# Output projection of a hybrid layer: where its sixteen-plus-sixteen units of work are issued among attention's rounds

## The reference, cut to what matters

```python
proj = h @ w_in[l]                                   # aq, ak, av, bu, bg, cq, ck, cv
out_a = _dilated_mixture(aq, ak, av)                 # 8 heads of 64
out_b = _conformer_conv(bu, bg, conv_w, ...)         # 31 taps over time, 512 channels, layer norm, silu
out_c, _ = _band_attention(cq, ck, cv, 127, sinks)   # 16 heads of 64
mix = concat([out_a, out_b, out_c])                  # 512 + 512 + 1024 = 2048 channels
x = x + mix @ w_out[l]                               # 2048 x 2048
h2 = _rms_norm(x, norm2_g[l])
x = x + (silu(h2 @ w_gate[l]) * (h2 @ w_up[l])) @ w_down[l]
```

## Time and profile before

| | |
|---|---|
| median of 3 runs | 2099.89 us (2097.58 to 2101.59) |
| the profiled execution's own time | 2101.12 us |
| its span, first to last instruction | 2099.4 us |
| mean granted TensorE clock | 0.987 |
| PE busy | 2032.4 us (97% of the span) |
| DVE busy | 1123.7 us (54%) |
| ACT busy | 932.1 us (44%) |
| DMA | 360.79 MB, mean 172 GB/s |

### The profile page before, as it was taken

One profiled execution on the slowest core, in us unless ns is written; L12 is line 12 of the kernel. 1 busy time (PEld: TensorE's weight loads), 2 busy tenths in 40 slices (PEclk: granted clock), 3 DMA queues, 4 the chain that ended last, 5 costly groups with the idle time before them and its releaser, 6 DMA issues.

```text
span 2099.4 us, 28004 instructions
## 1 busy us (share of the span) xinstructions
PE 2032.4 (97%) x10386; PEld 1721.1 (82%) x10386; DVE 1123.7 (54%) x1309; ACT 932.1 (44%) x1215; POOL 77.0 (4%) x126
## 2 busy tenths in 40 slices
PE   8999999998999999999999888999999999999998
PEld 6888988887879998887788766888888888888886
DVE  5474544655555453654656874555444544444443
ACT  5355434444454443444554424454444444433342
POOL 3000000001100000000200100000000000000000
PEclk9999999999999999999999998999999999999999
DMA  8574455565665444565554422566666666656653
GB/s 259 166 241 121 131 159 167 172 199 147 209 196 174 136 141 146 175 200 162 158 170 134 128 90 101 167 205 187 190 188 189 191 188 187 189 191 203 205 202 111
DMA packets 209513, 360.79 MB, mean 172 GB/s; under 512 B 22641, under 2 KB 45728, under 8 KB 209152
## 3 DMA queue, kind: packets, MB, share of 16 engines
q1 hardware_dynamic: 203728, 345.36, 53.7%
q0 software_dynamic: 4816, 13.76, 2.2%
q10 hardware_dynamic: 864, 0.26, 0.1%
HBM read 357.22 MB, written 2.10 MB: 171 GB/s over the span
## 4 chain that ended last, share of the span: by engine, by line
PE 92%; DVE 2%; ACT 2%; DMA 2%; issue 1%; SPq 1%; DVEq 0%; ACTq 0%; POOL 0%; POOLq 0%
PE psum L550 24%; PE psum L552 24%; PE psum L551 24%; PE psum L558 3%; PE psum L560 3%; PE psum L561 3%; PE psum L607 1%; PE psum L1181 1%; SPq L505 1%; PE psum L616 1%; DVE wl L521 1%; PE psum L779 1%; PE psum L856 1%; PE psum L630 1%; ACT wh L514 1%
## 5 line engine op out<-in xcount | busy, mean ns | idle before, releaser
L521 DVE TENSOR_TENSOR wl<-raw,wh 128x1024 fp32r<-128x1024 f32 (+2 forms) x672 | 797.9, 1197 | 734.3 <-ACT wh L514 727.2
L514 ACT ACTIVATE wh<-raw 128x1024 fp32r<-128x1024 f32 (+2 forms) x672 | 690.7, 1037 | 885.5 <-PE psum L552 716.1
L550 PE MATMUL psum<-wh,xh 128*128 128x512 f32 (+2 forms) x1600 | 623.7, 390 | 0.8 <-DVE xl L798 0.6
L552 PE MATMUL psum<-wh,xl 128*128 128x512 f32 (+2 forms) x1600 | 616.8, 385 | 0.0
L551 PE MATMUL psum<-wl,xh 128*128 128x512 f32 (+2 forms) x1600 | 616.4, 385 | 0.0
L550 PEld LDWEIGHTS psum<-wh,xh 128*128 128x128 f32 x1600 | 302.5, 189 | 62.1 <-DVE wl L521 1.9
L552 PEld LDWEIGHTS psum<-wh,xl 128*128 128x128 f32 x1600 | 301.6, 188 | 59.6
L551 PEld LDWEIGHTS psum<-wl,xh 128*128 128x128 f32 x1600 | 302.4, 189 | 57.6
L550 PE MATMUL psum<-wh,mh 128*128 128x512 f32 x384 | 154.0, 401 | 16.7 <-issue 8.5
L552 PE MATMUL psum<-wh,ml 128*128 128x512 f32 x384 | 152.6, 397 | 0.0
L551 PE MATMUL psum<-wl,mh 128*128 128x512 f32 x384 | 152.5, 397 | 0.0
(11 more groups left out here) (340 smaller groups left out, 1550.0 us busy)
## 6 DMA issues: line engine op xcount, KB each, us to landing
raw<-in_w_in_dram SPq DMA_DIRECT2D x264, 512.0 KB, 4.4
raw<-in_w_out_dram SPq DMA_DIRECT2D x96, 512.0 KB, 3.7
raw<-in_w_gate_dram SPq DMA_DIRECT2D x88, 512.0 KB, 3.6
raw<-in_w_up_dram SPq DMA_DIRECT2D x88, 512.0 KB, 3.6
raw<-in_w_down_dram SPq DMA_DIRECT2D x80, 512.0 KB, 3.7
bias<-in_b_in_dram POOLq DMA_DIRECT2D x18, 256.0 KB, 4.0
raw<-in_w_in_dram SPq DMA_DIRECT2D x16, 268.0 KB, 2.8
raw<-in_nsa_cmp_w_k_dram SPq DMA_DIRECT2D x32, 128.0 KB, 2.5
```

Source lines behind the costliest of these rows:

```text
L514: act.activation(wh[:, n % SPLIT_SLOTS, 0:k, 0:unit.n], raw[:, n % RAW_SLOTS, 0:k, 0:unit.n], ACT.Copy).then_inc(hi_done, 1)
L521: dve.tensor_tensor(out=wl[:, n % SPLIT_SLOTS, 0:k, 0:unit.n], in0=raw[:, n % RAW_SLOTS, 0:k, 0:unit.n], in1=wh[:, n % SPLIT_SLOTS, 0:k, 0 ...
L550: pe.matmul(o, ah_[:, kt, tok], hi_w, start=first, stop=False)
L552: ins = pe.matmul(o, al_[:, kt, tok], hi_w, start=False, stop=last)
```

## The change

The order in which the 32 units of `w_out` are issued is new. All four column groups take their pairs 4 to 7 first ("early"), are added to `x`, and take pairs 0 to 3 in a second pass ("late"), which is added to `x` again. Slots 16 to 28 then hold 2, 2, 3, 1, 3, 2, 2, 3, 4, 2, 4, 2 and 2 units, one slot fewer than before; slots 16 to 22 hold 15 and the first of slot 23 is the sixteenth early one. There are eight `add_output` instead of four. In slot 23 the wait for mid 22 is on the second unit, in slot 24 the wait for mid 23 on the first. `turn_final_x` for the last columns moves from stage 28 to 27. The taps of the convolution are spread otherwise (31 before and after), and `head_scale` of the `aq` and `ak` groups moves from mid 11 and 13 to mid 12 and 14, with `sinks_max` put first in mids 11 and 13.

```diff
 def output_slots_2():
-    def unit(g, pair):
-        return output_unit("w_out_2", g, pair, 3, 4)
-    rest = [output_unit("w_out_2", g, pair, 7) for g in (2, 3) for pair in range(8)]
-    slots = [[unit(0, 4)], [unit(0, 5)], [unit(1, 4), unit(1, 5)], [unit(0, 6)], [unit(0, 7), unit(1, 6)], [unit(1, 7)],
-             [], [unit(0, 0), unit(0, 1), unit(1, 0), unit(1, 1)], [unit(0, 2), unit(0, 3)],
-             [unit(1, 2), unit(1, 3), rest[0], rest[1]]]
-    slots[7][0].after_mid = 22
+    def early(g, *pairs):
+        return [output_unit("w_out_2", g, pair, 7, 4) for pair in pairs]
+
+    def late(g, *pairs):
+        return [output_unit("w_out_2", g, pair, 3, 0) for pair in pairs]
+    slots = [early(0, 4, 5), early(1, 4, 5), early(0, 6, 7) + early(1, 6), early(1, 7), early(2, 4, 5, 6),
+             early(2, 7) + early(3, 4), early(3, 5, 6), early(3, 7) + late(0, 0, 1), late(0, 2, 3) + late(1, 0, 1),
+             late(1, 2, 3), late(2, 0, 1, 2, 3), late(3, 0, 1), late(3, 2, 3)]
+    slots[7][1].after_mid = 22
     slots[8][0].after_mid = 23
-    slots[9][2].after_mid = 24
-    return slots + slots_of(rest[2:])
+    return slots
...
-                26: lambda: turn_final_x(range(0, 8)), 28: lambda: turn_final_x(range(8, EARLY_KT)),
+                26: lambda: turn_final_x(range(0, 8)), 27: lambda: turn_final_x(range(8, EARLY_KT)),
...
-                26: lambda: final_x_high(range(0, 8)), 28: lambda: final_x_high(range(8, EARLY_KT)),
+                26: lambda: final_x_high(range(0, 8)), 27: lambda: final_x_high(range(8, EARLY_KT)),
...
-            taps_at_unit = {first_tap_unit + SLOT_UNITS * i + n: 1 for i, m in enumerate((4, 4, 3, 3, 3)) for n in range(m)}
-            taps_at_mid = {9: 2, 15: 3, 16: 4, 17: 2, 18: 3}
+            taps_at_unit = {first_tap_unit + SLOT_UNITS * i + n: 1 for i, m in enumerate((4, 2, 3, 2, 3, 2, 2)) for n in range(m)}
+            taps_at_unit[first_tap_unit + sum(len(slot) for slot in SLOTS_2[11:19])] = 1
+            taps_at_mid = {9: 3, 15: 1, 16: 3, 17: 2, 18: 3}
...
-                11: lambda: (head_sums("aq2", 512), sinks_max("c10", 8), head_scale("aq2", 1, 512, split_heads(aqn)), sinks_sum("c10")),
-                12: lambda: (dve_copy_half(probT2)),
-                13: lambda: (head_sums("ak2", 512), sinks_max("c14", 12), small_out(o_c[1], 0), head_scale("ak2", 0, 512, split_heads(akn)), sinks_sum("c14")),
-                14: lambda: (dve_copy_half(probT2)),
+                11: lambda: (sinks_max("c10", 8), head_sums("aq2", 512), sinks_sum("c10")),
+                12: lambda: (dve_copy_half(probT2), head_scale("aq2", 1, 512, split_heads(aqn))),
+                13: lambda: (sinks_max("c14", 12), small_out(o_c[1], 0), head_sums("ak2", 512), sinks_sum("c14")),
+                14: lambda: (dve_copy_half(probT2), head_scale("ak2", 0, 512, split_heads(akn))),
...
-                17: lambda: (softmax_max("a0"), softmax_sum("a0")), 18: lambda: dve_copy_half(probT2),
-                19: lambda: (softmax_max("a4"), small_out(o_a, 0), softmax_sum("a4")),
-                20: lambda: (dve_copy_half(probT2), conv_mean()), 21: lambda: small_out(o_a, 4),
-                22: lambda: (conv_sumsq(), dve_mix_low(place, "a", mh2, ml2, 0, 0)), 23: conv_low,
-                24: lambda: add_output(0), 25: lambda: add_output(1), 26: lambda: final_x_low(range(0, 8), 1),
-                27: lambda: add_output(2), 28: lambda: final_x_low(range(8, EARLY_KT), 2), 29: last_output,
+                17: lambda: (softmax_max("a0"), softmax_sum("a0")),
+                18: lambda: (dve_copy_half(probT2), add_output(0)),
+                19: lambda: (softmax_max("a4"), small_out(o_a, 0), softmax_sum("a4"), add_output(1)),
+                20: lambda: (dve_copy_half(probT2), conv_mean()), 21: lambda: (small_out(o_a, 4), add_output(2)),
+                22: lambda: (conv_sumsq(), dve_mix_low(place, "a", mh2, ml2, 0, 0)),
+                23: lambda: (conv_low(), add_output(3)),
+                24: lambda: add_output(0), 25: lambda: add_output(1),
+                26: lambda: (add_output(2), final_x_low(range(0, 8), 1)),
+                27: lambda: final_x_low(range(8, EARLY_KT), 2), 28: last_output,
```

## The result

The changed kernel took 2085.54 us, the median of four runs (2084.14 to 2087.65), against 2100.74 for the kernel before: a ratio of 0.9931, 95% interval 0.9918 to 0.9944, or 12 to 17 us less. Measured again on another occasion, with five more runs of it, the ratio was 0.9917 (0.9904 to 0.9931). The forecast was 2085.5.

A forecast was written before the change was run, and what follows sets the result against it. PE, busy 97% of the span, was taken as the bound. Gains and losses at ten places summed to -14.4 us, taking the profiled 2101.12 to 2086.7, or 2085.5 against the median 2099.89; range 2080 to 2093.

The forecast's parts named there:

- (a): Slot 11: a third tap after mid 9 stands ahead of DVE's first split, so PE starts later; 1.7 us lost.
- (b): Stage 12 and slot 13: gap 0.9 us instead of 5.6, clock stays up; loss 8.5 before, 1.5 after.
- (c): Slot 17: its unit's wait and slow work go; 6.4 us lost before, 0 after.
- (d): Stage 18: DVE's work ahead of it outlasts PE's; gap 1.5 us instead of 0.9.
- (e): Slot 19: gap of 3.3 us and slow unit of 2.7 unchanged; mid 18's new addition fits under the slow unit.
- (g): Stage 22: two units now cover mid 21; gap of 1.2 us and about 1.4 of low clock go, gain 2.6.
- (h): Slot 23: its first unit covers mid 22; gap of 2.5 us and 1.9 of slow work go, gain 4.4.
- (i): Slot 24: uncovered mid 23 grows by a fourth split and an addition; gap 8.4 us for 6.0, 2.4 lost.
- (j): Stage 27: slot 27's two units do not cover mid 26, where four did before; 1.3 us lost.
- rival 2: More is won: slot 19's slow unit (2.7 us) may go and slot 11's tap (1.7) cost nothing; 2081, chance 0.09.
- rival 1: DVE, busier by four additions and the moved scaling, is late at more places, giving back 6.2 us; 2092, chance 0.11.
- rival 4: Slower: after the longer gap before slot 24 the clock stays low through slots 24 to 28; 2119 us, chance 0.04.

The follow-up runs named there:

- e6: The changed kernel with the third tap after mid 9 moved into slot 12: 2085.35 us, ratio 0.9925.
- e3: The changed kernel with mids 11 to 14 as before (head_sums ahead of sinks_max, head_scale in mids 11 and 13): 2087.45 us, ratio 0.9942.
- e2: The changed kernel with mids 9 and 11 to 14 and the taps of slots 11 to 15 as before, keeping the new unit order and additions: 2091.18 us.
- e11: The changed kernel without the four early add_output, so the early halves of the output projection are missing: 2082.3 us, ratio 0.9918.
- r1: The changed kernel, unedited, measured again: 2083.14 us, ratio 0.9917.
- e10: The changed kernel with the wait for mid 22 on slot 23's first unit instead of its second: 2088.98 us, ratio 0.9949.
- e4: The changed kernel with slot 24's fourth unit moved to slot 25 and add_output(3) ahead of conv_low: 2083.29 us, ratio 0.9922.
- e7: The changed kernel with the two taps after mid 17 moved to slots 14 and 15: 2084.46 us, ratio 0.9927.
- e5: The changed kernel with early units dealt one each to slots 21 to 23, two to slot 24 before mid 23's wait, add_output(3) in mid 24: 2077.72 us.
- e1: The kernel before with only the change's early part (mids 9 and 11 to 14, taps of slots 11 to 15): 2098.7 us, ratio 0.9984.
- e9: The kernel of e5 with one of slot 24's two early units moved to the end of slot 23: 2080.46 us, ratio 0.9909.

## Why the prediction was right, step by step

The table sets the steps against the two profiles. "Measured" is how much later or earlier PE reached the next mark after the end of stage 10, with 2.72 a unit for units that now lie elsewhere, and then the differences. For example, slot 24 began at 1301.22 - 1136.90 = 164.3 with 12 of the 32 units done, and after at 1299.25 - 1136.65 = 162.6 with 18: -1.7 - 6 x 2.72 = -18.0, where the mark before it (stage 22) stood at -14.2.

| step, up to the mark | predicted | measured |
|---|---|---|
| (a), (b): to stage 13 | -5.3 | -4.3 |
| (c): to stage 17 | -6.4 | -6.6 |
| (d): to stage 18 | +0.6 | +0.4 |
| (e): to stage 19 | 0 | -1.7 |
| (f), (g): to stage 22 | -2.6 | -2.0 |
| (h), (i) and the clock from stage 22 on: to slot 24 | -2.0 | -3.9 |
| (j) and slots 24 to 28: to the last turn of x | +1.3 | +1.3 |
| sum | -14.4 | -16.7 |

Sorted by kind, the sum forecast 7.3 us less of standing still and 7.1 us less of slow or DVE-paced work. The two windows of the stretch show 7.1 and 9.7. So the gaps, which are what the edit sets, came out as forecast, and what was mis-sized is nearly all clock.

**(a)** held in size (a gap of 1.57 for 1.7). It stands in the sum as a cost beside (b), whose gap it shortens by as much, so the total is right; but there is nothing to win by undoing it. e6 shows this: DVE sets stage 12, and a tap ahead of it costs the same wherever it stands. So the second gain of rival 2, 1.7 us from this tap, was not there.

**(b)** held in its gap, 0.95 for 0.9, and the clock stayed up. Its pace in slot 13 was mis-sized: from stage 12 to stage 13 PE took 14.89 us before and 13.50 after, 1.4 gained for 2.3 in the sum. DVE's pace, put at 0.6, cost about 1.1. Part of this is a new wait on `wl` before the first unit of slot 13, small, but one of the signs that the prediction named for being wrong:

```profile
1166.99 0.50 PE L552 MATMUL psum<-wh,xh 128*128 128x512 f32 x1 [0.35 <-DVE wl L523]
```

The cover claimed for `head_scale` held too, since e3 undoes the move and no gap of slots 14 to 18 shrinks.

**(c)** held in result, and its working was a little too dark. DVE was expected 1.5 late at mid 15; it waited 0.22 for stage 15:

```profile
1211.54 0.88 DVE L1665 TENSOR_TENSOR o_c<-psum,small 128x128 f32<-128x128 f32 x4 [0.22 <-PE psum L1297]
...
1214.03 1.68 DVE L757 SCALAR_TENSOR_TENSOR conv_y<-conv_h,conv_wT,conv_y 128x256 f32<-128x256 f32 x4
1215.78 1.23 DVE L523 TENSOR_TENSOR wl<-raw,wh 128x1024 fp32r<-128x1024 f32 x1
```

Most of that came from mid 13, which the sum had not used: it ended at 1192.7 for 1198.6 before, 5.9 earlier, where PE's stage 13 came only 4.6 earlier. e2 shows that (c) and what follows stand without the early part.

**(d)** came out at 1.41 for 1.5. **(e)** was mis-sized: the gap is 3.26 as forecast, but the slow unit was charged as certain, and in the profile of after it did not come (granted clock 1.00). With the unit at full clock PE was at stage 19 before mid 18 was done, the 0.66; the addition that was to hide under the slow unit showed, and e11 without it has no such gap. In r1 the unit was slow and the gap gone. This is rival 2's first half, by luck of the execution and not by the schedule.

**(g), (h)** held in their gaps, which are gone. e10 brings (h) back: a gap of 2.53 and a clock of 0.68 over 5.21 us of matmuls, 1.7 lost, together 4.2 for the 4.4 forecast (its stretch is 3.8 longer, as the clock behind slot 24's gap came back sooner in that execution). **(i)** held: 8.20 for 8.4, and e4 and e11 take its two halves out again, 2.07 together and 1.14 the addition. ACT and then DVE in the profile after show the chain as forecast, the fourth split ahead of the table load and the addition behind `conv_low`:

```profile
1291.15 1.06 ACT L516 ACTIVATE wh<-raw 128x1024 fp32r<-128x1024 f32 x1 [0.39 <-PE psum L554]
1292.22 1.28 ACT L1567 ACT_TABLE_LOAD   x1
```

```profile
1296.76 1.22 DVE L1665 TENSOR_TENSOR ml<-conv_sq,mh 128x1024 fp32r<-128x1024 f32 x1 [0.84 <-ACT mh L1571]
1297.90 1.22 DVE L1665 TENSOR_TENSOR x<-psum,x 128x1024 f32<-128x1024 f32 x1
```

**(j)** held: 1.08 for 1.3. The rows of (f) to (i) together gave -5.9 for -4.6. Of these 1.3 us, 0.2 is (i)'s shorter gap and 0.3 a wait of 0.27 before stage 20 that the sum did not list; some 0.8 is not placed.

The rivals: rival 1 is not what happened, but its ground was real: DVE has almost nothing to spare from slot 11 to mid 18, and work put ahead of a mark there comes back as a wait of PE (e6, e7). Rival 3 fell with the gaps. Rival 4 fell: after the 8.20 us gap the clock was back within some 5 us in both executions. The windows of r1 are shown above, those of the profile after are:

```profile
1299.20:1302.00 2.80, 2.75 (x7) 0.50 0.46 176
1302.00:1304.50 2.50, 2.50 (x9) 0.63 0.00 0
```

The loss there was thus 2.3 us, and 1.5 in r1, where the prediction charged 2.65 as in the kernel before.

Why the median moved by 15 and the profile's stretch by 16.7 is settled only in part. The profiled execution of the changed kernel was the fastest of its four, 1.4 us under their median; the intervals reach from 12 to 17 us, and in r1's comparison from 14.5 to 20; and the clock differs between executions of one kernel.

## What to carry to other kernels

When the bound engine's gaps come from another engine's queue, first ask which queue sets each mark: moving work inside that queue ahead of the same mark changes nothing (e6), and moving it ahead of an earlier mark mostly moves the wait (e7), while moving independent work of the bound engine under the wait removes it (e5, 8 us of stretch for no extra instruction). Cover is worth most where the chain has none at all; the change gave two units each to mids that needed 2 to 3 us and left the chain of 8 us bare. Splitting an accumulation in two passes is what made units free to move; its price here was four additions of 1.2 us, of which 1.8 us showed.

## What the runs showed of the hardware that was not expected

The gap before slot 19 was 3.26 or 3.27 us in twelve profiles of eleven kernels, and the granted clock over the 2.7 us after it was 0.50 in three of them (before, e1, e2), 0.55 in e3, 0.75 to 0.78 in e4, e6, e9 and r1, and 1.00 in after, e5, e10 and e11. The same program, after and r1, shows both. The Trainium skill (TensorE: Matmul & The Clock Gate, Part 1: The HAM clock gate) says that the count of slow matmuls at a kernel's start changes from run to run of one kernel; the traces show the same behind a gap in its middle. So the slow unit after a gap of this length is to be priced as a chance, not as a sum: 0 to 2.7 us here. After the gaps of 6.0 to 8.2 us before slot 24 the low clock came every time, in eleven profiles: 0.50 for 2.8 us at least, and 5.3 us in the kernel before and e1, whose gap of 6.02 is the shortest of them.

Shorter gaps were no protection. A low clock stood behind 2.53 us in e10 (0.68 over the next 5.3 us) and behind 2.33 in e3 (0.64 over 4.7), but not behind 2.70 in e6 (1.00). In the kernel before it stood even behind the 1.21 before stage 22. The window of PE there:

```profile
1275.40:1280.00 4.60, 4.47 (x16) 0.63 0.39 121
```
